# The reads of tiles that turn through DRAM: issued by GpSimd when their writes land, in place of SyncE two slots later

## The reference

```
hn = rmsnorm(x, norm_g[i])
y  = mixer(hn)          # differential attention, sliding window, mLSTM, differential attention
x  = x + y
```

```
# differential attention, 8 heads, two score maps each
q, k, v, g = split(hn @ w_in);  q, k = rope(q), rope(k)
p = softmax(q1 k1') - lam * softmax(q2 k2')      # causal
o = rmsnorm(p v) * silu(g);  y = o @ w_out
# mLSTM, 8 heads: a = (q k') * decay weights; h = a v / max(|sum a|, exp(-m)); rmsnorm(h) * sigmoid(o) * silu(g)
```

## Time and profile before

| | us |
|---|---|
| median of 3 runs | 1712.66 (1712.31 to 1713.44) |
| profiled execution | 1712.57 |
| its span, first to last instruction | 1710.8 |
| PE busy | 1699.6 (99%) |
| DVE busy | 1188.9 (69%) |
| ACT busy | 911.4 (53%) |
| POOL busy | 38.9 (2%) |
| mean granted TensorE clock | 0.999 |
| DMA, mean over the span | 213 GB/s, 364.53 MB |

### The profile page before, as it was taken

How to read it: one execution, slowest core, us unless ns; L and a number is a source line. 1 busy time by engine, 2 the same in 40 slices (tenths; PEclk the granted TensorE clock), 3 DMA queues, 4 the chain that set the end, 5 groups by cost and what they waited for, 6 DMA issues and landing times.

```text
span 1710.8 us, 24445 instructions
## 1 busy us (share of the span) xinstructions
PE 1699.6 (99%) x7890; PEld 1417.7 (83%) x7890; DVE 1188.9 (69%) x1909; ACT 911.4 (53%) x1400; POOL 38.9 (2%) x99
## 2 busy tenths in 40 slices
PE   9999999999999999999999999999999999999998
PEld 7888888888888888888888888888888888888887
DVE  7767677775769888865656465656676676777756
ACT  7454555554656666655544545454554555455543
POOL 1000000000000000000000000000000000000000
PEclk9999999999999999999999999999999999999999
DMA  8768676766875555478998699966877686767673
GB/s 286 244 194 262 201 245 215 233 216 220 264 216 161 160 159 153 154 234 194 190 166 271 177 201 182 265 182 216 260 227 237 195 265 200 247 214 232 223 237 126
DMA packets 230035, 364.53 MB, mean 213 GB/s; under 512 B 14950, under 2 KB 80044, under 8 KB 229836
## 3 DMA queue, kind: packets, MB, share of 16 engines
q1 hardware_dynamic: 229536, 362.94, 73.5%
q0 software_dynamic: 48, 0.13, 0.1%
q10 hardware_dynamic: 380, 0.56, 0.1%
HBM read 335.79 MB, written 27.79 MB: 213 GB/s over the span
## 4 chain that ended last, share of the span: by engine, by line
PE 95%; DMA 2%; issue 1%; SPq 1%; DVE 1%; ACT 0%; DVEq 0%; POOLq 0%; POOL 0%; ACTq 0%
PE acc L1136 29%; PE acc L1137 29%; PE acc L1138 29%; PE tp L1102 1%; PE tp L1137 1%; PE tp L1136 1%; PE tp L1138 1%; DMA raw<-in_ml_w_in_dram 1%; PE sc L1137 1%; PE sc L1136 1%; PE sc L1138 1%; DMA xres<-in_x_dram 0%; DMA qs<-q_turning 0%; DMA q_turning<-scr 0%; PE sc L1162 0%
## 5 line engine op out<-in xcount | busy, mean ns | idle before, releaser
L2015 DVE TENSOR_TENSOR w_lo<-raw,w_hi 128x1024 fp32r<-128x1024 f32 x583 | 703.2, 1220 | 401.4 <-ACT w_hi L1074 399.0
L1074 ACT ACTIVATE w_hi<-raw 128x1024 fp32r<-128x1024 f32 x583 | 610.2, 1056 | 454.9 <-PE acc L1138 401.6
L1136 PE MATMUL acc<-w_hi,xt_hi 128*128 128x512 f32 x1824 | 715.3, 392 | 1.7 <-DVE w_lo L2015 1.0
L1138 PE MATMUL acc<-w_hi,xt_lo 128*128 128x512 f32 x1824 | 711.0, 390 | 0.0
L1137 PE MATMUL acc<-w_lo,xt_hi 128*128 128x512 f32 x1824 | 710.4, 389 | 0.0
L1138 PEld LDWEIGHTS acc<-w_hi,xt_lo 128*128 128x128 f32 x1824 | 342.4, 188 | 72.3
L1136 PEld LDWEIGHTS acc<-w_hi,xt_hi 128*128 128x128 f32 x1824 | 342.6, 188 | 70.3 <-DVE w_lo L2015 1.6
L1137 PEld LDWEIGHTS acc<-w_lo,xt_hi 128*128 128x128 f32 x1824 | 342.6, 188 | 67.3
L1136 PE MATMUL acc<-w_hi,ot_hi 128*128 128x512 f32 (+1 forms) x456 | 176.6, 387 | 0.0
L1138 PE MATMUL acc<-w_hi,ot_lo 128*128 128x512 f32 (+1 forms) x456 | 175.8, 386 | 0.0
L1137 PE MATMUL acc<-w_lo,ot_hi 128*128 128x512 f32 (+1 forms) x456 | 175.8, 385 | 0.0
(11 more groups left out here) (306 smaller groups left out, 1226.5 us busy)
## 6 DMA issues: line engine op xcount, KB each, us to landing
raw<-in_da_w_in_dram SPq DMA_DIRECT2D x255, 512.0 KB, 4.4
raw<-in_ml_w_in_dram SPq DMA_DIRECT2D x96, 512.0 KB, 5.7
raw<-in_sw_w_in_dram SPq DMA_DIRECT2D x72, 512.0 KB, 3.7
raw<-in_da_w_out_dram SPq DMA_DIRECT2D x64, 512.0 KB, 4.0
raw<-in_sw_w_out_dram SPq DMA_DIRECT2D x32, 512.0 KB, 3.7
raw<-in_ml_w_in_dram SPq DMA_DIRECT2D x64, 256.0 KB, 7.3
raw<-in_ml_w_out_dram SPq DMA_DIRECT2D x32, 512.0 KB, 3.9
qs<-q_turning SPq DMA_DIRECT2D x12, 512.0 KB, 6.9
```

Of the source, the lines that this page charges most:

```text
L1074: act.activation(w_hi[:, q:q + 2, :], raw[:, 2 * p:2 * p + 2, :], ACT.Copy).then_inc(hi_ready, 1)
L1136: pe.matmul(out_ap, k_hi, m_hi, start=start, stop=False)
L1138: return pe.matmul(out_ap, k_lo, m_hi, start=False, stop=stop)
L2015: dve.tensor_tensor(w_lo[:, two, :], raw[:, two, :], w_hi[:, q:q + 2, :].bitcast(F32), ALU.subtract).then_inc(lo_ready, 1)
```

## The change

`q_read`, `k_read`, `p_read` and `o_read` leave the tables, and `read` calls for them leave SP's program. POOL's loop of four iterations is written out, and each iteration has the reads in the order of the data: q, k, P, the inverse roots, output (q, root, output in mLSTM). POOL waits for the four writes of a tile (64 on its `_written` semaphore) and issues the same transfer, with the same landing tile and semaphore.

```diff
-DA = dict(q_evac=11, q_turn=12, q_write=19, q_read=21, q_copy=20, ... k_read=29, ... p_read=41, ... o_read=52, ...)
+DA = dict(q_evac=11, q_turn=12, q_write=19, q_copy=20, ...)
...
             def move_q(w, l):
...
-                if (i := w.due(when["q_read"])) is not None:
-                    read(flat(qs), q_dram, "q_written", in_iter(l, "q_written", i, 64), "q_moved")
...
+            def flat(tile):
+                return tile[:].rearrange("p t n -> p (t n)")
+
+            def read(l, i, tile, landing, rows):
+
+                pool.wait_ge(sig[f"{tile}_written"], in_iter(l, f"{tile}_written", i, 64))
+                pool.dma_start(landing, rows).then_inc(sig[f"{tile}_moved"], 16)
...
-                with pool.Fori(0, ITERS) as i:
-                    own.more = i * OWN_STEPS["pool", kind]
+                for i in range(ITERS):
+                    read(l, i, "q", flat(qs), q_dram)
                     if kind == "da":
+                        read(l, i, "k", shared[:, 0:T * JW], k_dram)
+                        read(l, i, "p", p_landed, p_dram)
                         for h in range(2):
                             pool.wait_ge(sig["ssq_done"], in_iter(l, "ssq_done", i, 2 * h + 2))
                             inverse_root(o_rs[:, h, :], o_ms[:, h, :], o_ss[:, h, :], S).then_inc(sig["o_rstd"], 1)
                     else:
-                        flat = [a[:].rearrange("p a b -> p (a b)") for a in (o_rs, o_ms, o_ss)]
                         pool.wait_ge(sig["ssq_done"], in_iter(l, "ssq_done", i, 4))
-                        inverse_root(*flat, S).then_inc(sig["o_rstd"], 1)
-                own.more = 0
-                own.n += (ITERS - 1) * OWN_STEPS["pool", kind]
+                        inverse_root(flat(o_rs), flat(o_ms), flat(o_ss), S).then_inc(sig["o_rstd"], 1)
+                    read(l, i, "o", flat(th), o_dram)
```

More of the change, by code:

```diff
@@ L64 @@
 MOVED = {"da": 4, "sw": 3, "ml": 4}
-DA = dict(q_evac=11, q_turn=12, q_write=19, q_read=21, q_copy=20, k_evac=19, k_turn=20, k_write=27, k_read=29, k_copy=28,
-          v_evac=27, score=25, softmax=29, diff=(31, 33), p_turn=34, p_write=39, p_read=41, p_copy=40, pv=(37, 38), ssq=(41, 42),
-          g_tanh=35, gate=36, mix=45, o_write=50, o_read=52, o_split=54, o_split_last=51)
+DA = dict(q_evac=11, q_turn=12, q_write=19, q_copy=20, k_evac=19, k_turn=20, k_write=27, k_copy=28,
+          v_evac=27, score=25, softmax=29, diff=(31, 33), p_turn=34, p_write=39, p_copy=40, pv=(37, 38), ssq=(41, 42),
+          g_tanh=35, gate=36, mix=45, o_write=50, o_split=54, o_split_last=51)
 SW = dict(kv_evac=3, sink_set=10, v_stage=14, k_T=5, k_hi=9, k_lo=(10, 13), q_evac=11, q_T=11, q_hi=(15, 16), q_lo=(15, 15, 17, 18),
@@ L73 @@
           o_gate=(26, 28), o_hi=(27, 29), o_lo=(29, 30))
-ML = dict(qk_evac=11, q_turn=12, q_write=17, q_read=19, qk_copy=19, score=(17, 18), decay=(18, 19), weigh=(21, 22),
+ML = dict(qk_evac=11, q_turn=12, q_write=17, qk_copy=19, score=(17, 18), decay=(18, 19), weigh=(21, 22),
           v_evac=19, pv=(20, 21), den=25, ssq=26, comb=29, o_tanh=27,
-          g_tanh=35, gate=36, mix=37, o_write=43, o_read=45, o_split=45)
+          g_tanh=35, gate=36, mix=37, o_write=43, o_split=45)
 COUNTS = {
@@ L587, in move_k @@
                     write(k_rows, qk_blocks["da"], "k_turned", in_iter(l, "k_turned", i, 1), "k_written")
-                if (i := w.due(DA["k_read"])) is not None:
-                    read(shared[:, 0:T * JW], k_dram, "k_written", in_iter(l, "k_written", i, 64), "k_moved")
             def move_p(w, l):
@@ L594, in move_p @@
                     write(p_rows, p_blocks, "p_turned", in_iter(l, "p_turned", i, 1), "p_written")
-                if (i := w.due(DA["p_read"])) is not None:
-                    read(p_landed, p_dram, "p_written", in_iter(l, "p_written", i, 64), "p_moved")
             def move_o(w, l):
@@ L602, in move_o @@
                     write(o_rows, o_blocks, "o_turned", in_iter(l, "o_turned", i, 1), "o_written")
-                if (i := w.due(when["o_read"])) is not None:
-                    read(flat(th), o_dram, "o_written", in_iter(l, "o_written", i, 64), "o_moved")
             def move_x(w):
```

## The result

The changed kernel takes 1726.74 us (median of 4, 1725.06 to 1728.82) against 1712.49: ratio 1.0083, 95% interval 1.0071 to 1.0094. It is **14 us slower**; 1711.6 was forecast. The profiled execution took 1728.82, its span is 1727.1, 16.3 above the span of before.

What follows compares the result with a forecast made beforehand. TensorE, idle only 11.2 us, was taken to bound the kernel. Profiled execution 1712.57 less 1.1 us of mLSTM stalls behind q's read gave 1711.5, plus 0.1 to the runs' median: 1711.6 us, range 1710.6 to 1715.0.

Steps and rivals of the forecast that it cites:

- What bounds the kernel: TensorE is busy 1699.6 of 1710.8 us; three waits in the body cap any gain at 1.9 us, 0.11%.
- What goes from SP: 40 reads and their waits leave SP's queue: value 0, at most the third loss of 0.76 us.
- What POOL gets: The 40 reads in the order of the data, nothing else due on POOL then: cost in the span 0.
- When the reads start: q's no sooner than 145.76; the output's 1.6 to 2 us sooner, taking 512 KB out of q's way.
- How long POOL's read takes: Issue to landing 6 us, bounds 3.4 and 9.7, against 6.9 at the median for q's read on SP.
- VectorE's copies: By the skill's rule an f32 copy locks out POOL's descriptor writing; one copy, 0.42 us, would make q's read 6.4 us.
- The cover in differential attention: Near slot 20 a later q costs TensorE only from 1.15 us on, a read over 8.7 us; at 6, 0.
- Rival 2: POOL's read of q is late in eight differential-attention iterations, 1.0 us each, 8 us in all: 1720.7; chance 0.07.
- Rival 3: In four mLSTM iterations reads overtake weight loads without slack, 8 x 0.76 = 6.1 us: 1718.8; chance 0.07.
- Rival 4: All three TensorE losses go, as SP no longer waits ahead of weight loads: 1710.8; chance 0.08.
- Rival 1: No gain: the losses come from full DMA engines in one of four equal iterations: 1712.6; chance 0.28.

Runs made afterwards that it cites:

- g1: Changed kernel, but SP waits until POOL has issued each read, and in differential attention POOL reads the output after the next q: 1713.12 us, ratio 0.9997.
- g2: Kernel before the change, but in mLSTM slots SP issues writes and reads of turned tiles ahead of the slot's weight load: 1714.20 us, ratio 1.0002.
- f1: Kernel before the change, nothing on POOL, but SP's mLSTM read of q moved from slot 19 to 21: 1721.13 us, ratio 1.0047.
- f2: Changed kernel, all reads on POOL, but SP waits at the old slots until POOL has issued each read: 1713.74 us, ratio 1.0008.
- e4: Kernel before the change, but POOL reads q and the output in the mLSTM layer only: 1718.00 us, ratio 1.0026.
- f3: Changed kernel, but in differential attention POOL reads the output after the next iteration's q: 1717.51 us, ratio 1.0032.
- f4: Changed kernel, but the output's read in differential attention brings only 128 of 1024 columns, 64 KB for 512 KB: 1717.33 us, ratio 1.0028.
- e1: Changed kernel, but the output's reads go back to SP at their old slots; q, k and P stay on POOL: 1719.46 us, ratio 1.0035.
- e2: Kernel before the change, but only the output's reads are on POOL; SP reads q, k and P at old slots: 1713.99 us, ratio 1.0003.
- e3: Changed kernel, all reads on POOL, but SP still waits at the old slots until each tile's writes have landed: 1719.61 us, ratio 1.0039.

## Why the prediction was wrong, step by step

*What bounds the kernel*: right. The ceiling of 1.9 us on any gain held; g1 and g2 are within 0.1% of before.

*What goes from SP*: this step failed, and it is the first of two. I valued the removed waits at 0 because ACT had its weights in time, and asked only whether the waits held weight loads back too long. I did not ask what the held loads would do to the read once let go. The waits were doing work: they kept the line ahead of q's read at two loads. Without them it is four, and q lands in 12.6 us (f1: 14.0 with SP's own read, f2: 7.4 with the wait restored to the read's issue). Price with its clock: 5 us (e4), where I had put a value of 0 and at best a gain of 0.76.

*What POOL gets*: right; nothing queued behind its waits stalled TensorE, and an issue takes 0.53 to 0.62 us.

*When the reads start*: the times came as forecast, the output's at 142.39 (142.4 was forecast), and q's 0.29 us behind the landing of its writes. The step that failed is what the earlier start does: I took that landing, 145.76, as given, and the output's move as "512 KB out of q's way". SP was issuing q's writes from 140.68 on; a read moved to 142.39 lies on top of them. In the six iterations that stall, the last of them lands 5.2 to 6.1 us after its issue instead of 3.1 to 3.4 (f3, f4 and e1 bring that back to 3.7 or less, but for one of 4.8 in f4). Every DMA that the moved one now runs beside had to be asked, the writes before as well as the read behind.

*How long POOL's read takes*: 6 was forecast, 6.6 is q's median: right where the line was short, off by a factor of two in the mLSTM stretch. By the round robin that I took from the Trainium skill (*DMA: Bandwidth & Descriptors*, "Queues, rings and completion order") the read should have overtaken SP's waiting loads. The trace does not bear this out: with four loads ahead POOL's read took 12.6 us and SP's own 14.0. The first packet of POOL's read (a packet is a piece of a transfer in the trace) moved 8.6 us after the issue (f2: 3.4), and the read landed at 1035.18, behind the first three loads and 0.4 us ahead of the fourth. VectorE's copies, which were to lock POOL out, cost nothing that shows: g1 has all 40 reads on POOL at a ratio of 0.9997.

*The cover in differential attention*: 1.15 us was about right. Counted from q's first write, q lands 1.4, 2.3 and 2.0 us later in the first layer and 0.5, 1.2 and 1.0 are lost, a cover of 0.8 to 1.2 (0.3 to 1.7 in the last layer). Where it lands about as soon as before (e2), nothing is lost.

*Rival 2* named the right place and, at 8 us, nearly the right sum (8.3 lost there), by the wrong mechanism: it wanted a read of over 8.7 us, and the reads took 6.5 to 6.8; the writes ahead were late. That the sums are so near is luck. I gave it 0.07 on POOL's one DMA of before, which says nothing of writes. *Rival 3* went the other way: waits for mLSTM weights fell from 34.4 to 9.2 us. *Rival 4* had SP's freedom as a gain; it was the loss. *Rival 1* called the crowded iteration of the mLSTM layer one of four; it is two, the first and the third. The clock, 3.8 us, stood in no sum.

## What to carry to other kernels

A queue's blocking wait is also a throttle: before taking it away, count what will be issued into the gap and what it will stand ahead of. When a transfer is moved to start sooner, look at every transfer in flight at its new time, those that its successor depends on above all. A second queue gave no right of way here; if reads must move to one, let the bulk queue wait until the read is issued (f2), not until it may be (e3).

## What the runs showed of the hardware

- A read of 512 KB on POOL's queue passed at most the last of SP's weight loads ahead of it: it took 12.6 us with four of them, 7.4 with two; on SP's own queue 14.0 and 7.8.
- Four 128 KB writes on SP's queue are slowed by a read on POOL's beside them, from 3.3 to 5.1 us; the same read cut to 64 KB leaves them at 3.4.
- POOL issues such a read in 0.53 to 0.62 us, and starts 0.29 us after the last write has landed; the 1.37 us of the earlier trace rows was no guide.
- After 5.2 and 2.7 us without work TensorE was granted half its clock for the next 5 and 3.5 us; after the stalls of up to 1.7 us it was not.
- In the first and the third mLSTM iteration (820 to 900 and 1000 to 1080 us) the DMA engines are full in every run, share 1.01 to 1.03, at 174 to 189 GB/s; in the second and fourth they are not (940 to 980 us: share 0.64 to 0.66 at 174 to 180). Why is open. All that a late q cost in that layer was lost in the third.
